# A hybrid decoder layer on eight cores: projections of the next head placed ahead of the scan, with two sets of buffers

## What is computed

```python
# retention, per head and chunk
sc = einsum('td,sd->ts', qc, kc) * intra
o  = einsum('ts,sv->tv', sc, vc) + einsum('td,dv->tv', qc, S) * q_decay
S  = S * state_decay + einsum('sd,sv->dv', kc * k_decay, vc)
# mLSTM, per head and chunk (b: running sum of the forget gate, m: running maximum)
sc  = einsum('td,sd->ts', qc, kc) * dw
num = einsum('ts,sv->tv', sc, vc) + iw * einsum('td,dv->tv', qc, C)
h   = num / max(abs(den), exp(-mt))
C   = sd * C + einsum('s,sd,sv->dv', sw, kc, vc)
```

## Time and profile before

| | us |
|---|---|
| median of 3 runs (2865.17 to 2871.86) | 2871.23 |
| the profiled execution | 2865.31 |
| its span on the slowest core (core 6) | 2863.8 |
| TensorE busy in it | 2355.7 (82%) |
| VectorE, ScalarE, GpSimd busy | 1011.2, 531.2, 456.2 |

### The profile page before, as it was taken

One profiled execution on the slowest core, in us unless ns is written; L12 is line 12 of the kernel. 1 busy time (PEld: TensorE's weight loads), 2 busy tenths in 40 slices (PEclk: granted clock), 3 DMA queues, 4 the chain that ended last, 5 costly groups with the idle time before them and its releaser, 6 DMA issues.

```text
span 2863.8 us, 42398 instructions; the slowest of 8 cores (2827.2 to 2863.8 us)
## 1 busy us (share of the span) xinstructions
PE 2355.7 (82%) x14978; PEld 1323.8 (46%) x15148; DVE 1011.2 (35%) x2325; ACT 531.2 (19%) x1265; POOL 456.2 (16%) x430
## 2 busy tenths in 40 slices
PE   0799928887797887868649659999999999999993
PEld 0567716453463534435214447744444444444441
DVE  0422115444434435352611911222323233232337
ACT  0111111322324323232400411110010100101013
POOL 1121012122021000000000533311010110101007
PEclk9999958797797777868569879999999999999996
DMA  7466283655636655452394093466565755646644
GB/s 89 71 68 67 30 115 60 140 70 139 123 72 151 118 86 106 81 110 43 97 208 74 1 140 51 63 66 75 67 73 69 72 69 65 76 65 66 78 55 149
DMA packets 376721, 244.72 MB, mean 85 GB/s; under 512 B 142434, under 2 KB 370930, under 8 KB 373794
## 3 DMA queue, kind: packets, MB, share of 16 engines
q0 software_dynamic: 299408, 148.59, 43.8%
q1 hardware_dynamic: 77106, 93.40, 11.3%
HBM read 346.30 MB, written 44.24 MB: 136 GB/s over the span
## 4 chain that ended last, share of the span: by engine, by line
PE 73%; DMA 14%; DVE 5%; issue 4%; ACT 2%; POOL 1%; POOLq 0%; SPq 0%; DVEq 0%; ACTq 0%
PE ps L1002 17%; PE ps L984 16%; PE ps L469 13%; PE ps L433 12%; PE ps L871 4%; PE ps L960 4%; DMA C_s<-arena 2%; DMA arena<-x_pre 2%; DMA arena<-x_own 2%; DMA arena<-st_ret 2%; DMA retS_s<-arena 1%; DMA arena<-w_out 1%; PE psx L723 1%; DVE arena L716 1%; DMA arena<-w_pe_gate 1%
## 5 line engine op out<-in xcount | busy, mean ns | idle before, releaser
L1002 PE MATMUL ps<-arena 128*128 128x512 bf16 (+1 forms) x2256 | 500.9, 379 | 3.7 <-issue 1.3
L984 PE MATMUL ps<-arena 128*128 128x512 bf16 (+1 forms) x3015 | 466.0, 308 | 3.3 <-issue 0.2
L433 PE MATMUL ps<-arena 128*128 128x512 bf16 (+1 forms) x1995 | 368.2, 337 | 14.3 <-DVE arena L446 4.3
L469 PE MATMUL ps<-arena 128*128 128x256 bf16 (+1 forms) x3328 | 369.8, 273 | 0.0
L1002 PEld LDWEIGHTS ps<-arena 128*128 128x128 bf16 (+1 forms) x2304 | 218.1, 97 | 282.6 <-issue 24.3
L469 PEld LDWEIGHTS ps<-arena 128*128 128x128 bf16 (+1 forms) x3328 | 321.8, 97 | 42.9 <-issue 1.9
L984 PEld LDWEIGHTS ps<-arena 128*128 128x128 bf16 x3072 | 226.5, 97 | 245.4 <-issue 3.8
L1006 DVE TENSOR_TENSOR arena<-arena,ps 128x512 f32<-128x512 f32 (+1 forms) x288 | 197.1, 686 | 283.7 <-PE ps L1002 283.7
L433 PEld LDWEIGHTS ps<-arena 128*128 128x128 bf16 x2048 | 166.1, 100 | 198.6 <-issue 44.0
L73 POOL DMA_DIRECT2D arena<-w_ff x100 | 104.8, 1050 | 866.6 <-PE ps L1002 483.3
L988 ACT ACTIVATE arena<-ps 128x512 f32<-128x512 f32 (+1 forms) x192 | 88.2, 459 | 815.6 <-PE ps L984 744.5
(11 more groups left out here) (192 smaller groups left out, 1931.9 us busy)
## 6 DMA issues: line engine op xcount, KB each, us to landing
arena<-w_in POOLq DMA_DIRECT2D x48, 1024.0 KB, 12.1
arena<-w_ff POOLq DMA_DIRECT2D x36, 1024.0 KB, 9.3
arena<-w_ff POOLq DMA_DIRECT2D x64, 512.0 KB, 7.8
arena<-st_ret SPq DMA_DIRECT2D x64, 256.0 KB, 3.4
retS_s<-arena SPq DMA_DIRECT2D x64, 256.0 KB
arena<-st_C SPq DMA_DIRECT2D x64, 256.0 KB, 2.9
C_s<-arena SPq DMA_DIRECT2D x64, 256.0 KB
arena<-x_own SPq DMA_DIRECT2D x4, 2048.0 KB, 11.4
```

The lines of the kernel that those rows point to most:

```text
L433: ins = e.matmul(ps[:, 0:n], W[:, dt, ct * 128:(ct + 1) * 128], XT[:, dt, t0:t0 + n], start=(dt == 0), stop=(dt == 15))
L469: ins = e.matmul(ps[0:np_, 0:ncols], XT[:, dt, tt * 128:tt * 128 + np_], W[:, dt, 0:ncols], start=(dt == 0), stop=(dt == 15))
L984: ins = e.matmul(ps[:, 0:n], W1[s][:, dt, :], X1T[:, dt, t0:t0 + n], start=(dt == 0), stop=(dt == 15))
L1002: ins = e.matmul(ps[0:np_, :], HT[:, fl, tt * 128:tt * 128 + np_], WB[s][:, fl, :], start=(fl == 0), stop=(fl == 7))
```

## The change

The head loop is split into two functions, `own_proj` and `own_scan`, and recorded as proj(0), then for each head proj(hh+1) and scan(hh). `QT`, `KT`, `VEXT` and `GATE` exist twice and alternate by the parity of the head. The banks are regrouped: one ring of 7 whose banks are also used for the bf16 transposes; the projections take banks 0 to 2 of it, everything of the scans (the transposes included) banks 3 to 6, and all other stages all 7. To make room, `SINIT` moves to DRAM: the prefix pass stores each head's initial state, and the scan loads it into `SF[0]` by a DMA on SyncE in place of the two copies on GpSimd; the sample n vectors are loaded and stored per mLSTM head (256 columns) in place of once for all.

```diff
-    PS = [nc.alloc_psum_tensor("ps%d" % i, [128, 512], F32) for i in range(5)]
+    PS = [nc.alloc_psum_tensor("ps%d" % i, [128, 512], F32) for i in range(7)]
     PSX = nc.alloc_psum_tensor("psx", [128, 512], F32)
-    PB = [nc.alloc_psum_tensor("pb%d" % i, [128, 1024], BF16) for i in range(2)]
+    RINGS = dict(all=[0, 1, 2, 3, 4, 5, 6], proj=[0, 1, 2], scan=[3, 4, 5, 6])
+    def bank(pool="all"):
+        r = RINGS[pool]
+        i = r[st[pool] % len(r)]; st[pool] += 1
         return PS[i], "PS%d" % i
+    def bbank(pool="all"):
+        t, k = bank(pool)
+        return t[:].bitcast(BF16), k
...
-    QT = AR.alloc([128, 2, TOK], BF16)
-    KT = AR.alloc([128, 2, TOK], BF16)
+    QTs = [AR.alloc([128, 2, TOK], BF16) for _ in range(2)]
+    KTs = [AR.alloc([128, 2, TOK], BF16) for _ in range(2)]
-    VEXT = AR.alloc([128, 9, 260], BF16)
-    GATE = AR.alloc([128, 9, 256], BF16)
-    SINIT = AR.alloc([128, 8, 2, 260], F32)
+    VEXTs = [AR.alloc([128, 9, 260], BF16) for _ in range(2)]
+    GATEs = [AR.alloc([128, 9, 256], BF16) for _ in range(2)]
+    SINIT_D = nc.dram_tensor("sinit_scratch", [8, 128, 2, 260], F32).ap()
...
     def proj_fm(W, wk, ct, t0, n):
-        ps, pk = bank()
+        ps, pk = bank("proj")
...
-    def make_ktok(c, scale_ap):
-        pb, pk = bbank()
+    def make_ktok(KT, kK, c, scale_ap):
+        pb, pk = bbank("scan")
...
+        P.dma("sp", SF[0][:, :, 0:257], SINIT_D[hh][:, :, 0:257], r=["SINITD%d" % hh], w=["SF0_0", "SF0_1"], sem="SF0ld")
         for j in range(2):
-            P.op("pool", lambda e, j=j, hh=hh: e.tensor_copy(SF[0][:, j, 0:257], SINIT[:, hh, j, 0:257]), r=["SINIT%d_%d" % (hh, j)], w=["SF0_%d" % j])
             P.op("act", lambda e, j=j: e.copy(SBF[0][:, j, 0:257], SF[0][:, j, 0:257]), r=["SF0_%d" % j], w=["SBF0_%d" % j])
...
-            pst, pks = bank()
+            pst, pks = bank("scan")
...
+    args = lambda hh: (hh, QTs[hh % 2], KTs[hh % 2], VEXTs[hh % 2], GATEs[hh % 2], hh % 2)
+    own_proj(*args(0))
+    for hh in range(8):
+        if hh < 7:
+            own_proj(*args(hh + 1))
+        own_scan(*args(hh))
```

More of the change, by code:

```diff
@@ L641, in build_program, with own_proj @@
     smp_ctr = [0]
-    for hh in range(8):
+    def own_proj(hh, QT, KT, VEXT, GATE, par):
+        kQ, kK, kV, kG = "QT%d_" % par, "KT%d_" % par, "VEXT%d_" % par, "GATE%d_" % par
         ret = hh < 4
@@ L647, in build_program @@
         if hh == 0:
-            nxtO = [load_w(q * 1024) for q in range(4)]
-        (Wq, wqk), (Wk, wkk), (Wv, wvk), (Wg, wgk) = nxtO
-        for (W, wk, DST, dk, sc) in ((Wq, wqk, QT, "QT", None), (Wk, wkk, KT, "KT", 0.0625)):
+            st["nxtO"] = [load_w(q * 1024) for q in range(4)]
+        (Wq, wqk), (Wk, wkk), (Wv, wvk), (Wg, wgk) = st["nxtO"]
+        for (W, wk, DST, dk, sc) in ((Wq, wqk, QT, kQ, None), (Wk, wkk, KT, kK, 0.0625)):
             for t0, n in ((0, 512), (512, 512), (1024, 16)):
@@ L682, in trs @@
             return ins
[L683 removed]
+        P.op("pe", trs, r=skeys + blk_keys(kK, 1024, 16), w=[pkb])
         if ret:
@@ L731, in build_program @@
             cb = slice(c * 128, (c + 1) * 128)
-            qk = blk_keys("QT", c * 128, 128); kk = blk_keys("KT", c * 128, 128)
-            pst, pks = bank()
+            qk = blk_keys(kQ, c * 128, 128); kk = blk_keys(kK, c * 128, 128)
+            pst, pks = bank("scan")
             def st_mm(e, pst=pst, c=c):
@@ L738, in st_mm @@
                 return ins
-            P.op("pe", st_mm, r=["KTOK%d" % c, "VEXT%d" % c], w=[pks])
+            P.op("pe", st_mm, r=["KTOK%d" % c, kV + "%d" % c], w=[pks])
             if not ret:
-                pn, pkn = bank()
+                pn, pkn = bank("scan")
                 def n_mm(e, pn=pn, c=c):
@@ L758, in build_program @@
             if ret:
-                ps, pk = bank()
+                ps, pk = bank("scan")
                 def sc_mm(e, ps=ps, cb=cb):
@@ L766, in build_program @@
                 P.op("dve", lambda e, ps=ps, h=h, SCM=SCM: e.tensor_tensor(SCM[:], ps[:, 0:128], RMASK[:, h, :], ALU.mult), r=[pk, "C"], w=[kscm])
-                po, pko = bank()
+                po, pko = bank("scan")
                 def o_mm(e, po=po, cb=cb, c=c, SCM=SCM, cur=cur):
@@ L780, in build_program @@
                 NUMER, knu = S["NUMER"], "NUMER%d" % sid
-                psa, pka = bank()
+                psa, pka = bank("scan")
                 P.op("pe", lambda e, psa=psa, c=c, h=h: e.matmul(psa[:, 0:128], AA[:, c, h:h + 1].to_broadcast([128, 128]), IDF, start=True, stop=True),
@@ L793, in build_program @@
                 P.op("dve", lambda e, ps=ps, SCM=SCM, DW=DW: e.tensor_tensor(SCM[:], ps[:, 0:128], DW[:], ALU.mult), r=[pk, kdw], w=[kscm])
-                pb, pkb = bbank()
+                pb, pkb = bbank("scan")
                 P.op("pe", lambda e, pb=pb, SCM=SCM: e.transpose(pb[:, 0:128], SCM[:], IDB), r=[kscm], w=[pkb])
                 copy_op("act", SCMT[:], pb[:, 0:128], r=[pkb], w=[kscmt])
-                pi, pki = bank()
-                P.op("pe", lambda e, pi=pi, c=c, SCMT=SCMT: e.matmul(pi[:, 0:257], SCMT[:], VEXT[:, c, 0:257], start=True, stop=True), r=[kscmt, "VEXT%d" % c, "VONE"], w=[pki])
-                pe_, pke = bank()
+                pi, pki = bank("scan")
+                P.op("pe", lambda e, pi=pi, c=c, SCMT=SCMT: e.matmul(pi[:, 0:257], SCMT[:], VEXT[:, c, 0:257], start=True, stop=True), r=[kscmt, kV + "%d" % c, ("VONE" if par == 0 else "VONE1")], w=[pki])
+                pe_, pke = bank("scan")
                 def in_mm(e, pe_=pe_, cb=cb, cur=cur):
```

79 lines of the change are left out of this document (40 added, 39 removed).

## The result

| | kernel before | changed kernel |
|---|---|---|
| median, us | 2871.15 (10 runs) | 3003.1 (10 runs) |
| ratio, 95% interval | | 1.0461 (1.0436 to 1.0486) |
| profiled execution, us | 2865.31 | 3000.41 |
| end of the own-chunk loop in it, us | 1446.69 | 1578.34 |

The change costs 132 us of the median; 2936 was forecast, in a range up to 3000. The direction was right, the size was twice what was worked out. Of the 135 us between the two profiled executions, 131.7 are in the own-chunk loop, so the forecast of nothing elsewhere held.

A forecast was written before the change was run, and what follows sets the result against it. The loop alternates TensorE-bound projections and scans bound by engine hops; longer bank cycles, stalls and head ends add 39 (retention), 19 (mLSTM) and 7.3 (last scan), +65 on 2865.3, plus 5.9 to the median: 2936 us. Range for 8 in 10: 2845 to 3000.

The forecast's parts named there:

- nothing elsewhere: Outside the own-chunk loop: prefix pass, dense stages and weight loads put at nothing (prefix pass 0 to 5 us).
- the token work in the retention cycle: Retention scan: one token update, 0.71 us, and its copy, 0.62, fall onto the chunk cycle, in a pace of 7.8.
- The two regimes: Own-chunk loop: projections are pure TensorE at clock 1.00; in the scan alone work hops between engines at clock 0.50.
- P = 61: Own-chunk loop: the projections of one head (v, gate, q and k) take 61 us.
- the planner keeps the projections in one block: Own-chunk loop: proj(hh+1) runs in one block, then scan(hh); about 1.7 us (0 to 14) of projection hidden.
- L469 in pieces: Sign in the trace: v and gate matmuls running in pieces, not one block, would make the prediction wrong.
- the banks, which cost: Scans on 4 banks: next chunk waits for the transpose's copy; pace 6.9 to 7.8 us (retention), 7.5 to 9.5 (mLSTM).
- the end of the head: mLSTM head end: n_p stores precede the new state load and L671 follows; 9.8 us (0 to 15).
- B: Rival, scans: the banks don't bind, paces stay 6.9 and 7.5 us; -16, so 2855; chance 0.17.
- C: Rival, scans: both cycles long, near 9.1 and 11.1 us, with all token work in the chain; about 3015; chance 0.16.
- A: Rival, own-chunk loop: real overlap, scan steps between projection groups, TensorE sets the pace; about 2653; chance 0.12.

The follow-up runs named there:

- x1_banks: The kernel before with only the PSUM banks regrouped (3 for projections, 4 for scans with their transposes): 2989.12 us, ratio 1.0402.
- x5: The changed kernel without the two n_p stores at the end of each mLSTM head: 2958.34 us, ratio 1.031.
- x6: The kernel before without the two n_p stores at the end of each mLSTM head: 2848.49 us, ratio 0.9916.
- x2_dram: The kernel before with only SINIT moved to DRAM and n loaded and stored per head: 2883.52 us, ratio 1.0036.
- x15_np_lat: The changed kernel with scans recorded first, gate function once per head, banks 2, 3 and 2, n_p buffer and other planner constants: 2816.22 us, ratio 0.9776.
- x16_before_np_lat: The kernel before, without overlap of heads, with the n_p buffer and other planner constants: 2818.57 us, ratio 0.9801.
- x4_tables: The changed kernel with the gate's Silu and Sigmoid replaced by a plain copy: 2971.15 us, ratio 1.035.
- x7_batch: The changed kernel with the gate's function done once per head behind all gate blocks: 2994.58 us, ratio 1.0405.
- x3_scanfirst: The changed kernel with scan(hh) recorded ahead of proj(hh+1): 2955.08 us, ratio 1.0291.
- x20_after_lat: The changed kernel with only the planner's constants changed: 2985.55 us, ratio 1.0376.
- x14_np: The changed kernel with scans recorded first, gate function once per head, banks 2, 3 and 2, and a separate n_p buffer: 2844.48 us, ratio 0.9883.
- x11_best: The changed kernel with scans recorded first, gate function once per head, and banks 2, 3 and 2: 2839.36 us in the profiled execution, no ratio.

## Why the prediction was right, and where it was wrong

The cause and the direction were right, and three steps fell short: that the projections stay in one block, the token work in the retention cycle, put at 1.33 us where it holds both tokens (7.8 us forecast, 8.9 measured), and the end of an mLSTM head, put at 9.8 us where stores and load took 29.7, 13.0 and 13.1.

- **What bounds what.** The two regimes held. The 60.6 us between scans 0 and 1 of after look like P = 61, but by luck, as said above.
- **Step "the planner keeps the projections in one block".** Right for retention heads. Wrong from the projections of head 4 on: L470 ran in groups of 16 from 896.31, within a retention scan. The prediction let every projection group wait behind the first that was held up by a buffer of the scan. But the planner holds no such queue: each bank hands on by itself, and a group whose bank and target are free goes ahead of one that isn't. This reading comes from the planner's rule; what the runs show is that the pieces come with the rings alone (x1_banks). The prediction named L469 in pieces as what would make it wrong. The pieces gained little; table loads and weights not yet there (11.65 us in the chain) came with them, but how much they took back wasn't measured.
- **Step "the banks, which cost".** The mechanism is shown: x1_banks alone +115, L774 released by L641, n by L641, and a ring of 5 and of 7 close the cycle at the step that the order of takes gives. The mLSTM cycle, 9.5 forecast, is 9.2. The retention cycle, 7.8 forecast, is 8.9: the term of the token work was sized at one update and one copy, 1.33, and holds both tokens of the chunk. 1.1 us by seven chunks by four heads are 31 of the 67 us that missed in all (an estimate, since not every interval is a bare cycle).
- **Step "the end of the head", 9.8.** It is 22.43 + 7.28 at the first mLSTM boundary and 9.20 + 3.75 at the second, 9.73 + 3.33 at the third. The stores were put at their duration in before, and the load behind them at nothing. But the load is in series with them, and TensorE can't fill the wait: at the first two boundaries the remaining projections stand in its list behind a step of the scan, and at the third there are none. x5 and x6 give the stores at 21 us over the kernel before.
- **By stage**: retention +67 where 39 were forecast, mLSTM +57 where 19 were, last scan +7.5 where 7.3 were. x1_banks, the rings alone, has +78, +29 and +7. So retention needs no other cause. In mLSTM the rings' 29 and the stores' 23 make 52 of the 57, if they add up; the first stores are as long in x1_banks (19.78 us), so the two overlap in part. Table loads, late weights and the order of recording are candidates for what is left.
- **The budget by experiments**: rings 115, state in DRAM 10, n_p 21, together 146, where 132 were lost. So the overlap that did happen gives back about 14, if these add up, and they do so only roughly: the stores wait in x2_dram and in x1_banks too.
- **The rivals.** B fell with x1_banks. C named the right reason for retention (all token work in the chain, 9.1) and the wrong size for mLSTM (11.1); its 3015 is nearer to 3003 than the forecast. A, 2653, was priced as if TensorE were all that stands in the way; x15_np_lat has the overlap, and its 2816 doesn't beat its control.
- **The rules quoted.** The Trainium skill, "Perfetto Trace Analysis", section Optimization Strategy, says that equal bubbles can mean too few buffers. Here the shared ring of 7 keeps them (9.1), and 3 with 2 apart, two banks fewer, nearly lose them (8.0); the number of buffers didn't decide. The same section says that interleaving regimes with different bounds may gain. In x15_np_lat against x16_before_np_lat this is so in the mLSTM heads (359.5 against 393.9), but not in the whole kernel (0.9776 against 0.9801, inside the intervals).

## What to carry to other kernels

When buffers are handed out round a ring, number the takes of one iteration and ask which step inherits the buffer of the last one: a ring that is longer can close a longer cycle, and a class of tiles that is freed late is better off in a ring of its own. In a chain in which all engines are in order, count every piece of side work that is queued between two steps of the cycle, not one of each kind. Before restructuring for overlap, try the constants of the planner that orders the work: here they gave more than the restructuring. And run the control without the restructuring: it showed that the restructured kernel was no faster for it, although one of its stages was.

## What the hardware showed that was not expected

The two stores of n_p, 128 single elements each, took 22.43 us from issue to landing at one place and 9.20 and 9.73 at others of the same kernel; what made the first so long isn't known, and I had taken 9.48 for a fixed price. It was the longest at the same place, behind the first mLSTM head, in x1_banks (19.78), x4_tables (16.65), x7_batch (23.04), x3_scanfirst (28.36) and x20_after_lat (26.12). Taking the stores out of the next state load's way made this load of 257 KB land after 9 to 11 us in place of 3.5 (x14_np against x11_best, second and third boundary). A change between the gate's function and those of the scan cost 1.283 us on ScalarE each time, with no exception in 52, and the next instruction began 0.01 us behind it; but removing 34 of them (with 18.6 us of other work put in) moved the median by no more than its interval.
